# Every fourth expert row of heads 0 to 2: from VectorE to ScalarE and GpSimd

## The chip, the cores and the metric

The kernel runs on one core of a Trainium2 chip. The core has five engines with a queue of instructions each: TensorE (PE in the profile, with its weight loads as PEld), VectorE (DVE), ScalarE (ACT), GpSimd (POOL) and SyncE (SP). They work side by side and meet at semaphores. The metric is the device time of one execution in microseconds (us); lower is better.

## The reference, cut to what matters

The layer is a decoder block: a mixer of attention heads and state-space heads, whose output is added to the residual `h`, and then a PEER channel mixer. For each of 512 tokens and each of 8 heads, PEER picks 16 of 16,384 experts. The picked rows of two tables are then used:

```
u   = expert_down[idx]                       # (tokens, heads, 16, 1024)
pre = einsum('bthkd,btd->bthk', u, xn)
act = gelu(pre) * gates                      # gates: softmax over the 16 picked
out = einsum('bthk,bthkd->btd', act, expert_up[idx])
h   = h + out                                # then a final RMSNorm
```

So each token needs 128 rows of each table, 4 KB each, all in float32. The two tables lie side by side in memory, and one row of the joined table is 8 KB.

## The kernel before, in words

The tokens are worked on in four tiles of 128, one token to a partition. A slot `s` is one picked expert for all 128 tokens of a tile: there are 128 slots to a tile, 16 to a head, 512 in all. GpSimd issues one indirect DMA for each slot (`gather(s)`, L378 to L411), which brings 128 rows of 8 KB, 1.05 MB, into one of ten row buffers (eleven from slot 60 on; `ROW_OF`). A buffer can be filled again when its last user is done with it, and `gather(s)` waits for that.

What happens to a row after it has landed:

- VectorE multiplies its down half by the normed tokens and sums (`dots`, L1049; the instruction is L1053).
- ScalarE takes the gelu of a group of slots (L605), VectorE multiplies by the gates (`gates`, L1058; L1065), and the factors are in `actv`.
- ScalarE makes a diagonal matrix of each factor (L616), and TensorE multiplies it by the up half of the row into the accumulators of the tile (`expert`, L1464; L1477). Its last matmul signals `row_free`.

In the first three heads (`OUT_HEADS` is 3, slots 0 to 47) the slots 3, 7, 11, ... 47 (`SHARE` is 4) take another way: `by_dve(s)` is true, ScalarE and TensorE skip them, and VectorE itself computes `h = row * actv + h` over 128x1024 (`add_row`, L1046). That ends with the signal `row_added`, on which the gather that reuses the buffer waits. It is issued from `dots` of the next group, right behind the first dot product of it. There are 12 such slots. They are in these heads because TensorE has other work there: the output projection of the mixer (`pieces`, L1416), which must end before the gathers of the query weights 5 to 7 begin (L325). The residual with the twelve rows in it is added to the accumulators much later (`add_residual`, L1505).

Head 0's gathers begin at 200 us of the span, while the mixer still runs. From head 3 on (slot 48) GpSimd also makes a diagonal for each slot (`gate_diagonal`, L419), between two gathers.

The order on each engine is written out by hand: what stands behind an instruction that waits, waits too. The names `ring`, `step_ps` and so on belong to the mixer and play no part here. All row buffers, diagonals and small tables are parts of three big tiles, `arena`, `arena2` and `wide`, so that the profile shows most operands under these names.

Of the kernel before, what the change touches and what calls it, by code (L numbers as in the profile page):

```python
# [74 lines left out]

def by_dve(s):

    return s < OUT_HEADS * TOPK and s % SHARE == SHARE - 1

DVE_DONE = list(itertools.accumulate(int(by_dve(s)) for s in range(NS)))
PE_DONE = [s + 1 - DVE_DONE[s] for s in range(NS)]

# [12 lines left out]
def layer(nc, x, x_t, w_in_blocks, w_vd, norm_mix, conv_w, conv_b, dt_bias, a_log, d_skip, ssd_norm_w, sinks, w_out,  # L96
          rel_bias, bucket_line, norm_ffn, w_query, keys1_t, keys2_t, experts_du, norm_cols, out):
    line_dram = nc.dram_tensor("line_scratch", (P, HEADS * LW), F32, kind="Internal").ap()
    with ExitStack() as ctx:
# [239 lines left out]
        def _(gp):  # L339
# [32 lines left out]
            def gate(c):  # L372
# [3 lines left out]
                link(gp, g.tensor_tensor(yb[:, c, :], yb[:, c, :], zs[c], ALU.mult), "gated", n)  # L376

            def gather(s):  # L378
                q, i = divmod(s, TOPK)
# [22 lines left out]
                if s == WIDER:  # L402
                    gp.wait_ge(sem("wo_half"), 2 * NT)
                elif user is not None:
                    if by_dve(user):
                        gp.wait_ge(sem("row_added"), DVE_DONE[user])
                    else:
                        gp.wait_ge(sem("row_free"), PE_DONE[user])
# [37 lines left out]
            gather(11)  # L446
            gather(12)
            gather(13)
            gather(14)
            gather(16)  # L450
            gather(15)
            gather(17)
            gather(18)
            gather(19)
            for s in range(20, NS):
                gather(s)
                if s - 2 >= OUT_HEADS * TOPK:
                    gate_diagonal(s - 2)
# [5 lines left out]
        def _(act):  # L464
# [137 lines left out]
            def group(s0, n_slots):  # L602
                part = slice(s0 % 16, s0 % 16 + n_slots)
                act.wait_ge(sem("dots"), s0 + n_slots)
                nc.scalar.activation(gel[:, part], pre[:, part], ACT.Gelu).then_inc(sem("gelu"), 1)  # L605
                act.wait_ge(sem("act_ready"), N_BEFORE[s0] + 1)
                if s0 == 0:
                    act.wait_ge(sem("off_ps"), NT - 1)
                if s0 == TOPK:
                    act.wait_ge(sem("gated"), 2)  # L610
                for s in range(s0, s0 + n_slots):
                    if by_dve(s):
                        continue
                    if s >= 8:
                        act.wait_ge(sem("row_free"), PE_DONE[s - 8])
                    nc.scalar.activation(diag(s), ident[:], ACT.Copy, scale=actv[:, s % 16:s % 16 + 1]  # L616
                                         ).then_inc(sem("diag"), 1)
# [154 lines left out]
        def _(dve):  # L772
# [266 lines left out]

            def add_row(s):  # L1040

                t = s // SLOTS
                if DVE_DONE[s] > 1:
                    dve.wait_ge(sem("row_added"), DVE_DONE[s] - 1)
                dve.wait_ge(sem("act_ready"), GROUP_OF[s] + 1)
                v.scalar_tensor_tensor(h[:, t, :], rows[ROW_OF[s]][:, D:2 * D], actv[:, s % 16:s % 16 + 1], h[:, t, :],  # L1046
                                       ALU.mult, ALU.add).then_inc(sem("row_added"), 1)

            def dots(s0, n_slots):  # L1049
                for s in range(s0, s0 + n_slots):  # L1050
# [3 lines left out]
                                           pre[:, s % 16:s % 16 + 1]).then_inc(sem("dots"), 1)  # L1054
                    if s == s0 and s and by_dve(s - 1):
                        add_row(s - 1)

# [163 lines left out]
        def _(pe):  # L1221
# [261 lines left out]
            def experts(s0, n_slots):  # L1483
                for s in range(s0, s0 + n_slots):
                    if not by_dve(s):
                        expert(s)
# [18 lines left out]
            def add_residual(t):  # L1505
                pe.wait_ge(sem("h_mixed"), 2 * t + 2)
                if t == 0:
                    pe.wait_ge(sem("row_added"), DVE_DONE[-1])
                for b in range(2):
# [205 lines left out]
```

## Time and profile before

| | |
|---|---|
| median of 3 runs | 1527.85 us (1527.29 to 1528.53) |
| the profiled execution, its own time | 1526.34 us |
| its span, first to last instruction | 1524.5 us |
| PE busy | 1325.1 us, 87% |
| DVE busy | 1053.0 us, 69% |
| ACT busy | 441.6 us, 29% |
| POOL busy | 1108.3 us, 73% |
| mean rate of the DMA engines | 374 GB/s |

The profile is of one execution. Busy shares are means over stages that differ: the mixer fills the first 200 us, and the experts the rest. The profile gives the rate of the DMA engines for 40 equal slices of 38.1 us, and for any stretch that is asked for. Times in the rows are us from the start of the span.

### The profile page before, as it was taken

How to read it: one execution, taken by the hardware profiler on the slowest of the kernel's cores; microseconds unless marked ns; L12 is line 12 of the kernel's file. 1: busy time of each engine (PE TensorE's matmuls, PEld its weight loads, DVE VectorE, ACT ScalarE, POOL GpSimd, SP SyncE). 2: the span in 40 equal slices, each digit the busy share in tenths (PEclk: the TensorE clock that was granted, in tenths of full speed). 3: DMA queues.
4: the chain of work that ended last, by engine and by line, in shares of the span. 5: the costliest groups of instructions: out<-in, count | busy, mean ns of one | idle time of the engine just before them, and what ended most of it. 6: DMA issues, size and time to landing. Idle time of an engine off the chain costs nothing.

```text
span 1524.5 us, 14446 instructions
## 1 busy us (share of the span) xinstructions
PE 1325.1 (87%) x4392; PEld 678.5 (45%) x4392; DVE 1053.0 (69%) x2534; ACT 441.6 (29%) x1216; POOL 1108.3 (73%) x1005
## 2 busy tenths in 40 slices
PE   8999998899888998889889898889888878888886
PEld 5557974444444443444444443434444334434432
DVE  3546598886776777677766676777777676667664
ACT  2123462122323232233223222233233222222222
POOL 0001134548899898888999998888999888888893
PEclk9999999999999999999999999999999999999999
DMA  7640069999999999999999999999999999999995
GB/s 254 172 184 12 1 259 413 412 418 422 421 420 422 421 421 422 421 421 421 421 421 418 421 416 422 422 421 409 408 421 423 420 422 422 421 421 421 416 415 231
DMA packets 85217, 569.80 MB, mean 374 GB/s; under 512 B 10227, under 2 KB 12564, under 8 KB 18708
## 3 DMA queue, kind: packets, MB, share of 16 engines
q0 software_dynamic: 73728, 536.90, 85.1%
q1 hardware_dynamic: 11412, 31.99, 6.2%
q8 instruction: 34, 0.56, 0.1%
q14 instruction: 43, 0.35, 0.1%
HBM read 565.19 MB, written 3.67 MB: 373 GB/s over the span
## 4 chain that ended last, share of the span: by engine, by line
DMA 32%; PE 30%; POOL 21%; DVE 10%; issue 4%; ACT 3%; SPq 0%; DVEq 0%; ACTq 0%; POOLq 0%
DMA arena<-in_experts_du_dram,arena 27%; PE ps L1477 14%; POOL arena L419 11%; POOL arena L409 8%; PE ps L1245 5%; DMA wide<-in_experts_du_dram,arena 5%; PE ps L1416 3%; DVE arena L1053 3%; PE ps L1451 3%; POOL wide L409 2%; ACT arena L647 1%; DVE wide L1053 1%; ACT arena L468 1%; PE ps L1260 1%; PE ps L1232 1%
## 5 line engine op out<-in xcount | busy, mean ns | idle before, releaser
L1477 PE MATMUL ps<-arena 128*128 128x512 f32 x1624 | 774.7, 621 | 141.6 <-ACT arena L647 133.0
L409 POOL DMA_INDIRECT arena<-in_experts_du_dram,arena x418 | 488.0, 1168 | 120.1 <-issue 63.8
L1477 PEld LDWEIGHTS ps<-arena 128*128 128x128 f32 x1624 | 307.3, 196 | 565.7 <-issue 329.9
L419 POOL TENSOR_SCALAR arena<-ident,arena 128x128 f32<-128x128 f32 x464 | 494.8, 1066 | 47.5 <-PE ps L1477 31.9
L1053 DVE CUSTOM_DVE_ANT_0 arena<-arena,wide 128x1024 f32<-128x1024 f32 x210 | 255.3, 1229 | 138.3 <-DMA arena<-in_experts_du_dram,arena 137.5
L1053 DVE CUSTOM_DVE_ANT_0 arena<-arena 128x1024 f32<-128x1024 f32 x208 | 252.6, 1228 | 114.8 <-DMA arena<-in_experts_du_dram,arena 114.1
L643 ACT ACTIVATE arena<-arena 128x2 f32<-128x2 f32 (+1 forms) x234 | 47.5, 203 | 762.0 <-DVE arena L1053 761.7
L1477 PE MATMUL ps<-wide,arena 128*128 128x512 f32 x376 | 183.2, 610 | 29.8 <-ACT arena L647 26.1
L647 ACT ACTIVATE arena<-arena 128x128 f32<-128x128 f32 x464 | 161.1, 394 | 8.1 <-ACT arena L643 0.2
L409 POOL DMA_INDIRECT wide<-in_experts_du_dram,arena x94 | 107.5, 1144 | 60.9 <-DVE arena L1037 24.0
L1477 PEld LDWEIGHTS ps<-wide,arena 128*128 128x128 f32 x376 | 70.0, 194 | 124.8 <-issue 73.6
L357 POOL TENSOR_TENSOR wide<-arena,hrow 128x512 f32<-128x512 f32 x4 | 4.7, 1170 | 116.0 <-ACT arena L468 115.9
L1245 PE MATMUL ps<-arena 128*128 128x512 f32 x192 | 83.4, 593 | 0.0
L1451 PEld LDWEIGHTS ps<-arena,wide 128*128 128x128 f32 x640 | 74.4, 192 | 8.9 <-issue 8.9
L1053 DVE CUSTOM_DVE_ANT_0 wide<-wide 128x1024 f32<-128x1024 f32 x46 | 56.6, 1230 | 30.1 <-DMA wide<-in_experts_du_dram,arena 30.0
L1451 PE MATMUL ps<-arena,wide 128*128 128x128 f32 x640 | 74.8, 275 | 0.0
L1053 DVE CUSTOM_DVE_ANT_0 wide<-wide,arena 128x1024 f32<-128x1024 f32 x48 | 58.8, 1225 | 23.1 <-DMA wide<-in_experts_du_dram,arena 22.9
L468 ACT ACTIVATE arena<-ps 128x256 f32<-128x256 f32 (+1 forms) x109 | 48.6, 446 | 48.0 <-PE ps L1460 14.4
L1416 PE MATMUL ps<-wide,arena 128*128 128x512 f32 x128 | 56.9, 593 | 1.1 <-DVE h L974 1.1
L1245 PEld LDWEIGHTS ps<-arena 128*128 128x128 f32 x192 | 36.1, 190 | 44.3 <-issue 44.2
L1451 PEld LDWEIGHTS ps<-arena 128*128 128x128 f32 x384 | 44.7, 192 | 6.0 <-issue 6.0
L1451 PE MATMUL ps<-arena 128*128 128x128 f32 x384 | 44.9, 275 | 0.6 <-ACT arena L468 0.6
(197 smaller groups left out, 1028.4 us busy)
## 6 DMA issues: line engine op xcount, KB each, us to landing
arena<-in_w_in_blocks_dram SPq DMA_DIRECT2D x16, 512.0 KB, 9.5
arena<-in_experts_du_dram,arena POOLq DMA_INDIRECT x418, 16.4
wide<-in_w_query_dram SPq DMA_DIRECT2D x5, 1024.0 KB, 9.3
wide<-in_w_out_dram SPq DMA_DIRECT2D x1, 4096.0 KB, 17.8
h<-in_x_dram SPq DMA_DIRECT2D x4, 512.0 KB, 9.7
arena<-in_w_query_dram SPq DMA_DIRECT2D x2, 1024.0 KB, 6.4
arena<-in_x_t_dram SPq DMA_DIRECT2D x3, 512.0 KB, 6.5
line_scratch<-arena SPq DMA_DIRECT2D x1, 1536.0 KB
```

The source lines that it names most:

```text
L409: gp.indirect_dma_start(rows[b], None, experts_du, bass.IndirectOffsetOnAxis(ap=idx[:, (q // PH) % 2, q % PH * TOPK + i:q % PH * TOPK + i ...
L419: g.tensor_scalar(diag(s), ident[:], eg[:, q % 2, i:i + 1], None, ALU.mult).then_inc(sem("gate_diag"), 1)
L468: link(act, nc.scalar.activation(o, i, func, **kw), name, n)
L643: nc.scalar.activation(gel[:, part], pre[:, part], ACT.Gelu).then_inc(sem("gelu"), 1)
L647: nc.scalar.activation(diag(s), diag(s), ACT.Copy, scale=gel[:, s % 16:s % 16 + 1]).then_inc(sem("diag"), 1)
L1053: v.tensor_tensor_reduce(down, down, xn2[s // SLOTS % 2], 1.0, 0.0, ALU.mult, ALU.add, pre[:, s % 16:s % 16 + 1]).then_inc(sem("dots"), 1)
L1232: last = mm(ps[0][:, t * P:(t + 1) * P], ring[:, 0, k, :], xnT[:, t, k, :], start=(k == 0), stop=(k == KT - 1))
L1245: last = mm(bank[:].rearrange("p (t c) -> p t c", t=NT), ring[:, ring_slot(b), k, :], xnT[:, :, k, :], start=(k == 0), stop=(k == KT - 1))
L1260: last = mm(ps[z_bank(t)][:, i * P:(i + 1) * P], xnT[:, t, k, :], ring[:, ring_slot(NXB + 5 + i), k, :], start=(k == 0), stop=(k == KT - 1))
L1416: ins = mm(ps[out_bank(c, b)][:], mixT[c][:, k, :], wo[:, k, b * 512:(b + 1) * 512], start=(k == 0), stop=(k == KT - 1), skip_group_check= ...
L1451: last = mm(ps[query_bank(q)][:, j * P:(j + 1) * P], w[:, k, j, :], xn2T[:, k, :], start=(k == 0), stop=(k == KT - 1))
L1477: last = mm(acc(t, b)[:], diag(s), up[:, b * 512:(b + 1) * 512], start=(s % SLOTS == 0), stop=False, skip_group_check=True)
```

## The change

The twelve rows are scaled by ScalarE in their buffer (a Copy with a scale, 128x1024), which signals `up_scaled`; GpSimd then adds the scaled row to `h` (a tensor_tensor, 128x1024) and signals `row_added`. VectorE's `add_row` is gone. `by_dve` and `DVE_DONE` are renamed.

```diff
-def by_dve(s):
+def by_pool(s):
     return s < OUT_HEADS * TOPK and s % SHARE == SHARE - 1
...
+            def add_row(s):                       # on GpSimd
+
+                t = s // SLOTS
+                gp.wait_ge(sem("up_scaled"), POOL_DONE[s])
+                gp.wait_ge(sem("h_mixed"), 2)
+                link(gp, g.tensor_tensor(h[:, t, :], h[:, t, :], rows[ROW_OF[s]][:, D:2 * D], ALU.add), "row_added", n)
...
             gather(12)
+            add_row(3)
             gather(13)
...
             gather(15)
+            add_row(7)
             gather(17)
...
             for s in range(20, NS):
                 gather(s)
+                if by_pool(s + 1 - RING_E):
+                    add_row(s + 1 - RING_E)
                 if s - 2 >= OUT_HEADS * TOPK:
                     gate_diagonal(s - 2)
...
                 for s in range(s0, s0 + n_slots):  # group(), on ScalarE
-                    if by_dve(s):
+                    if by_pool(s):
+                        up = rows[ROW_OF[s]][:, D:2 * D]
+                        nc.scalar.activation(up, up, ACT.Copy, scale=actv[:, s % 16:s % 16 + 1]
+                                             ).then_inc(sem("up_scaled"), 1)
                         continue
...
-            def add_row(s):                       # on VectorE
-                t = s // SLOTS
-                if DVE_DONE[s] > 1:
-                    dve.wait_ge(sem("row_added"), DVE_DONE[s] - 1)
-                dve.wait_ge(sem("act_ready"), GROUP_OF[s] + 1)
-                v.scalar_tensor_tensor(h[:, t, :], rows[ROW_OF[s]][:, D:2 * D], actv[:, s % 16:s % 16 + 1], h[:, t, :],
-                                       ALU.mult, ALU.add).then_inc(sem("row_added"), 1)
...
                     v.tensor_tensor_reduce(down, down, xn2[s // SLOTS % 2], 1.0, 0.0, ALU.mult, ALU.add,
                                            pre[:, s % 16:s % 16 + 1]).then_inc(sem("dots"), 1)
-                    if s == s0 and s and by_dve(s - 1):
-                        add_row(s - 1)
```

GpSimd's queue before, from the gather of slot 15 to that of slot 21 (in these rows `row_free` is TensorE's signal for a buffer, `row_added` that of the twelve rows):

```order
L409 DMA arena2<-in_experts_du_dram,arena 128x2048 [waits row_free]
L409 DMA arena<-in_experts_du_dram,arena 128x2048 [waits row_added]
L409 DMA arena<-in_experts_du_dram,arena 128x2048 [waits row_free] x2
L409 DMA wide<-in_experts_du_dram,arena 128x2048 [waits row_free]
L409 DMA arena<-in_experts_du_dram,arena 128x2048 [waits row_added]
```

The same piece of the queue now; L416 is the gather, L383 the addition of a row:

```order
L416 DMA arena2<-in_experts_du_dram,arena 128x2048 [waits row_free]
L383 TENSOR_TENSOR h<-h,arena 128x1024 [waits h_mixed,up_scaled]
L416 DMA arena<-in_experts_du_dram,arena 128x2048 [waits row_added]
L416 DMA arena<-in_experts_du_dram,arena 128x2048 [waits row_free] x2
L416 DMA wide<-in_experts_du_dram,arena 128x2048 [waits row_free]
L383 TENSOR_TENSOR h<-h,arena 128x1024 [waits h_mixed,up_scaled]
L416 DMA arena<-in_experts_du_dram,arena 128x2048 [waits row_added]
```

The rows of slots 7 and 11 are now added on GpSimd itself, each right ahead of the gather that reuses its buffer (slots 17 and 21), and the other gathers stand behind them.

Farther on, GpSimd's queue before, from the gather of slot 48 (it waits `routed`, the indices of the next head) to the diagonal of slot 49; L419 is a diagonal:

```order
L409 DMA arena<-in_experts_du_dram,arena 128x2048 [waits row_free,routed]
L409 DMA arena<-in_experts_du_dram,arena 128x2048 [waits row_added]
L409 DMA wide<-in_experts_du_dram,arena 128x2048 [waits row_free]
L419 TENSOR_SCALAR arena<-ident,arena 128x128 [waits row_free,gates_ready]
L409 DMA arena<-in_experts_du_dram,arena 128x2048 [waits row_free]
L419 TENSOR_SCALAR arena<-ident,arena 128x128 [waits row_free]
```

And the same piece now, up to the gather of slot 53; L426 is a diagonal:

```order
L416 DMA arena<-in_experts_du_dram,arena 128x2048 [waits row_free,routed]
L383 TENSOR_TENSOR h<-h,arena 128x1024 [waits h_mixed,up_scaled]
L416 DMA arena<-in_experts_du_dram,arena 128x2048 [waits row_added]
L416 DMA wide<-in_experts_du_dram,arena 128x2048 [waits row_free]
L426 TENSOR_SCALAR arena<-ident,arena 128x128 [waits row_free,gates_ready]
L416 DMA arena<-in_experts_du_dram,arena 128x2048 [waits row_free]
L426 TENSOR_SCALAR arena<-ident,arena 128x128 [waits row_free]
L416 DMA arena<-in_experts_du_dram,arena 128x2048 [waits row_free]
L383 TENSOR_TENSOR h<-h,arena 128x1024 [waits h_mixed,up_scaled]
L426 TENSOR_SCALAR arena<-ident,arena 128x128 [waits row_free,row_added]
L416 DMA arena<-in_experts_du_dram,arena 128x2048 [waits row_added]
```

The rows of slots 39 and 43 are added here, behind the gathers of slots 48 and 52; a third addition (slot 47) stands behind the gather of slot 56.

On ScalarE the scaling (L625) stands behind the three diagonals (L630) of its group, and ahead of the next gelu (L616):

```order
L616 ACTIVATE arena<-arena 128x4
L630 ACTIVATE arena<-ident,arena 128x128 x3
L625 ACTIVATE arena<-arena 128x1024
L610 ACT_TABLE_LOAD
L610 ACTIVATE arena<-arena 128x16
L616 ACT_TABLE_LOAD
```

## Rows read from the trace of the kernel before

**Rows 1.** The page: rate of the DMA engines in 40 slices; the gathers' queue.
```profile
GB/s 254 172 184 12 1 259 413 412 418 422 421 420 422 421 421 422 421 421 421 421 421 418 421 416 422 422 421 409 408 421 423 420 422 422 421 421 421 416 415 231
...
q0 software_dynamic: 73728, 536.90, 85.1%
```
**Rows 2.** The page, DMA issues: count, median us from issue to landing.
```profile
arena<-in_experts_du_dram,arena POOLq DMA_INDIRECT x418, 16.4
```
**Rows 3.** Stretches of 2 us: PE, PEld, DVE, ACT, POOL busy, PEclk, DMA share, GB/s.
```profile
264.00:266.00 2.00, 2.00 (x6) 0.83 (x5) 1.73 (x5) 0.90 (x4) 1.27 (x2) 1.00 0.95 299
266.00:268.00 2.00, 2.00 (x6) 0.88 (x5) 2.00 (x4) 0.29 (x1) 1.22 (x2) 1.00 0.93 385
268.00:270.00 2.00, 2.00 (x6) 0.95 (x5) 1.10 (x3) 0.00 (x0) 1.39 (x3) 1.00 0.91 307
270.00:272.00 2.00, 1.67 (x4) 0.38 (x2) 0.88 (x2) 0.00 (x0) 1.70 (x2) 1.00 1.01 348
...
328.00:330.00 2.00, 2.00 (x6) 0.95 (x5) 1.90 (x4) 0.49 (x2) 0.93 (x1) 1.00 1.02 365
```
**Rows 4.** Long stretches, L409 alone: gathers' time (count), PEclk, DMA share, GB/s.
```profile
195.00:263.25 68.25, 24.67 (x22) 0.97 0.89 357
...
195.00:334.49 139.49, 55.30 (x50) 0.98 0.95 384
195.00:341.20 146.20, 59.18 (x53) 0.98 0.95 386
```
**Rows 5.** Timeline of SyncE's DMA queue: query weights.
```profile
193.56 0.80 SPq L319 DMA_DIRECT2D arena<-in_w_query_dram  x2
288.75 0.86 SPq L323 DMA_DIRECT2D arena<-in_w_query_dram  x2
```
**Rows 6.** The chain that ended last: start, us, what.
```profile
245.20 9.56 DMA arena<-in_experts_du_dram,arena
254.79 1.24 DVE arena L1053 x2
...
259.40 5.41 PE ps L1477 x8
...
305.87 1.25 DVE arena L1053 x2
...
308.78 0.23 DVE arena L1065
...
309.49 7.11 PE ps L1477 x12
```
**Rows 7.** GpSimd's timeline: start, us, line, [idle before it, until what].
```profile
253.41 0.94 POOL L409 DMA_INDIRECT arena<-in_experts_du_dram,arena  x1 [0.30 <-issue]
263.25 1.10 POOL L409 DMA_INDIRECT arena<-in_experts_du_dram,arena  x1 [8.90 <-PE ps L1477]
...
330.74 0.94 POOL L409 DMA_INDIRECT arena<-in_experts_du_dram,arena  x1 [1.72 <-DVE arena L1037]
```
**Rows 8.** Line L1046, the removed addition: ns min/median/max, first and last start.
```profile
L1046 DVE SCALAR_TENSOR_TENSOR h<-arena,h x12: 1273/1280/1382, 230.8 to 343.1; 128x1024 f32<-128x1024 f32 x12
```
**Rows 9.** Tile h: ScalarE over 128x1024, same columns.
```profile
L468 ACT ACTIVATE wide<-h x2: 1040/1040/1041, 406.1 to 1052.1; 128x1024 f32<-128x1024 f32 x2
```
**Rows 10.** Groups on GpSimd: busy us, mean ns | idle before and releasers.
```profile
L376 POOL TENSOR_TENSOR wide<-wide,arena 128x512 f32<-128x512 f32 x4 | 5.1, 1271 | 40.9 <-DVE arena L819 34.5 <-DVE wide L928 6.4
L357 POOL TENSOR_TENSOR wide<-arena,hrow 128x512 f32<-128x512 f32 x4 | 4.7, 1170 | 116.0 <-ACT arena L468 115.9
```
**Rows 11.** GpSimd's timeline at 98 us.
```profile
97.91 1.04 POOL L357 TENSOR_TENSOR wide<-arena,hrow 128x512 f32<-128x512 f32 x1 [94.70 <-ACT arena L468]
```
**Rows 12.** VectorE's timeline over the same time.
```profile
98.03 1.47 DVE L884 TENSOR_TENSOR arena<-arena,dtv 128x512 f32<-128x512 f32 x1
99.53 0.69 DVE L888 TENSOR_TENSOR arena<-arena,dec 128x512 f32<-128x512 f32 x1
```
**Rows 13.** Line L419, GpSimd's diagonals: ns min/median/max.
```profile
L419 POOL TENSOR_SCALAR arena<-ident,arena x464: 593/793/2524, 336.4 to 1501.9; 128x128 f32<-128x128 f32 x155
```

More of the change, by code:

```diff
@@ L73 @@
 LOADS_IN_RING = [1 + sum(ring_slot(i) == ring_slot(n) for i in range(n)) for n in range(NBLK)]
-def by_dve(s):
+def by_pool(s):
     return s < OUT_HEADS * TOPK and s % SHARE == SHARE - 1
-DVE_DONE = list(itertools.accumulate(int(by_dve(s)) for s in range(NS)))
-PE_DONE = [s + 1 - DVE_DONE[s] for s in range(NS)]
+POOL_DONE = list(itertools.accumulate(int(by_pool(s)) for s in range(NS)))
+PE_DONE = [s + 1 - POOL_DONE[s] for s in range(NS)]
 ROW_OF = [s % RING_E if s < WIDER else (s - WIDER - 1) % (RING_E + 1) for s in range(NS)]
@@ L404, in gather @@
                 elif user is not None:
-                    if by_dve(user):
-                        gp.wait_ge(sem("row_added"), DVE_DONE[user])
+                    if by_pool(user):
+                        gp.wait_ge(sem("row_added"), POOL_DONE[user])
                     else:
@@ L1484, in experts @@
                 for s in range(s0, s0 + n_slots):
-                    if not by_dve(s):
+                    if not by_pool(s):
                         expert(s)
@@ L1507, in add_residual @@
                 if t == 0:
-                    pe.wait_ge(sem("row_added"), DVE_DONE[-1])
+                    pe.wait_ge(sem("row_added"), POOL_DONE[-1])
                 for b in range(2):
```

## The prediction, made before the run

> **What bounds the kernel now.** I read the DMA rate over the whole span first. From the seventh slice (229 us) to the last but one it stands at 408 to 423 GB/s [rows 1], and no engine is as full as that. Of the 569.8 MB of the page 536.9 MB are the gathers' 512 rows of 1.05 MB [rows 1], 2.49 us each at 422 GB/s. The kernel is a stream of DMA with compute beside it: a microsecond costs time when the DMA engines have nothing asked of them, and a delay elsewhere costs nothing as long as requests are queued. In the long middle a gather lands 16.4 us after it is issued (median) [rows 2], so six or seven rows are queued, and four or five microseconds of delay on GpSimd would pass unseen.
>
> The change acts only in slots 0 to 47, from 230 to about 355 us. There I looked for the stretches in which the rate falls. In steps of 2 us there are two: 264 to 272 us with 299, 385, 307 and 348 GB/s instead of 422, and 328 to 330 us with 365 [rows 3]. The first is (123 + 37 + 115 + 74) x 2 / 422 = 1.7 us lost, the second 0.3 us. All that a better feeding of the queue could win here is 2.0 us.
>
> Why the first is there, the chain of waits says [rows 6]: a row issued at 245.2 lands at 254.8, its dot product ends at 256, a search follows, TensorE starts the experts of slots 12 to 14 at 259.4, and only then is the buffer for slot 22 free. GpSimd issues slot 21 at 253.4, waits 8.9 us for TensorE and issues slot 22 at 263.25 [rows 7]. How full the queue was follows from two counts: by 263.25 us 68.25 us x 357 GB/s = 24.4 MB had moved [rows 4], and asked were 22 gathers (23.1 MB) and two blocks of query weights (2.1 MB) [rows 4, 5]. 0.8 MB, 1.9 us, was left. The same count gives 2.0 MB at 334.5 us (50 gathers and three blocks against 139.5 us x 384 GB/s) and 2.3 MB at 341.2 us [rows 4, 5], 4.8 and 5.4 us of work: nowhere near the 16 us of later.
>
> **What goes.** VectorE loses 12 additions of 1.28 us, 15.4 us [rows 8]. Does an end hang on them? The rows of the chain wait in turn for a row's landing (254.8 us) and for TensorE (309.5 us and on, which works through pieces and experts without a pause). The additions stand ahead of those waits, so VectorE would be early and wait longer. I count 0, and 2.0 us gained as the end of the range, if earlier gates keep the queue full at both dips.
>
> **What is added on ScalarE.** 12 scalings of 128x1024, 1.04 us each by the nearest row [rows 9], 12.5 us. They stand behind the diagonals that TensorE needs and ahead of a gelu that waits for VectorE's next dot products; ScalarE is 29% busy. I count 0; were one to stand in front of a gelu it would be 1.0 us at that place.
>
> **What is added on GpSimd.** 12 tensor_tensors of 128x1024 with both inputs in SBUF. The trace has none of that size. 128x512 took 1.27 us with two full inputs and 1.04 at best with a broadcast one [rows 10, 11]; twice that is 2.1 to 2.54 us, and I take 2.4. The Trainium skill's GPSIMD Engine Reference (section "Performance versus the Vector engine") has 4497 ns for 2048 elements, which would be an estimated 2.25 us for half of them; places 1, 2 and 4 would be some 0.15 us cheaper for each addition, half a microsecond in all.
>
> That is the bare price. The dearer part is that such an addition and VectorE hold each other up. At 97.91 us GpSimd starts a tensor_tensor of 1.04 us, and VectorE's two-input instruction of 98.03 us takes 1.47 us, where the next one of the same shape takes 0.69 [rows 11, 12]: 0.78 us longer, and it ends 0.55 us behind GpSimd's. The other way round, GpSimd's diagonals take 0.59 us at best, 0.79 in the median and up to 2.52 [rows 13], so one can wait nearly 1.9 us. The dot products (down half and tokens) and the gates have two SBUF inputs as well. So an addition can last 2.4 to 4.3 us in its queue, and stop VectorE for up to 2.4 us where it begins first. The Trainium skill's page SBUF — State Buffer, section "Who interferes with whom", states it as a lock: a VectorE instruction with two SBUF inputs and a GpSimd instruction that reads SBUF exclude each other, and the second blocks until the first ends; the trace agrees at 98 us, with its 0.78 us.
>
> Against the 1.28 us saved on VectorE thus stand up to 2.4 us of blocked VectorE for each row, and 2.4 to 4.3 us of GpSimd's queue, in which the gathers stand. By place:
>
> 1. The addition of slot 11, behind the gather of slot 20. It stands where slot 21 was issued before, at 253.41 [rows 7]; slot 7's addition ahead of it, less what GpSimd's waits for TensorE take up of it, shifts it by my estimate to 254 to 255.5 us. The dot product that the chain needs starts at 254.79 [rows 6]. If the addition is first, the dot product, the gates and slot 22 come about 1.9 us later, with an empty queue: 1.9 us. If the dot product is first, nothing, since a search of one-input instructions follows. I take 1.0.
> 2. The addition of slot 15, between the gathers of slots 24 and 25, in the stretch from 268 us. Slot 25 and the ones behind it come 2.4 us later, in the stretch that is already starved (307 and 348 GB/s). 0 to 2.4 us; since slots 22 to 24 are queued by then, 0.7.
> 3. The addition of slot 31, behind the gather of slot 40, by my estimate near 307 us. The gates that start TensorE's long run stand at 308.78, the dot product before them ends at 307.1 [rows 6]. An addition that begins there ends at 309.4: 0.6 us late; up to 1.7. TensorE then runs without a pause until slot 48, and slot 46, whose issue comes just before the second dip, goes with it. I take 0.6.
> 4. The additions of slots 39, 43 and 47, behind the gathers of slots 48, 52 and 56 (the first at 330.74 us [rows 7], the last by 354). GpSimd is now full: three additions of 2.4 to 3.2 us in front of diagonals and gathers, 7 to 10 us, against 4.8 and 5.4 us queued. Slot 49 would be issued at 334.4 to 336.3 us (330.74 + 0.94 + 0.3 + 2.4 to 4.3) instead of 332. From the 2.0 MB the 3 us take 1.3, and the next additions the rest; when the projection's pieces end, three query weights of 1 MB fill the queue again. 0 to 3 us; I take 1.3.
>
> The earlier additions (slots 3 and 7) delay slots that wait for TensorE anyway or have two rows queued before them: 0, up to 0.5 each. The others (slots 19, 23, 27, 35) fall where three to five rows are queued: 0.
>
> Sum: 1.0 + 0.7 + 0.6 + 1.3 = 3.6 us. Ends: -2.0, and 1.9 + 2.4 + 1.7 + 3.0 + 1.0 = 10 us if all go wrong. A loss here is not won back, because from 355 us on the DMA rate is at its top. Against the profiled execution's own 1526.34 us (span 1524.5 and 1.8 around it) this is 1529.9; the median of the runs is 1.5 us above that execution, so 1527.85 + 3.6 = 1531.5 us.
>
> **Rivals.** (a) The additions are absorbed. For it: only about 2 MB short of full anywhere, and the dips of before cost 1.7 and 0.3 us although the queue was nearly dry, so small gaps are cheap. Against it: place 4 asks more of GpSimd than it has. Time: 0 to 2.5 us more, about 1528.8. (b) VectorE's relief reaches the dip at 264 us: with three additions fewer before 256 us the gates of slots 12 to 15 come up to 1.28 us earlier, slot 22 too, and the queue does not run dry. It decides if the dot product at 254.79 was late for VectorE's sake; the row says it waited for a landing, which speaks against it. Price: -1.3 us, with the second dip -2.0, so 1525.9 to 1526.6. Only with an unforeseen gain of the same kind would it be seen as faster. (c) The blocking is stronger than I took: each of 12 additions waits the full 1.9 us and blocks VectorE for 2.4, places 1 to 4 all at their upper end: 1536 to 1538. (d) That the twelve rows still go through VectorE is excluded by the order.
>
> **How the numbers follow.** Forecast 3 to 7 us slower: 0.45. Rival (a): 0.38. Rival (b): 0.10. Rival (c): 0.07. A measurement of this kernel can tell 0.2%, 3.1 us, from no change. Slower by more than that: nearly all of the forecast's case and (c), 0.50. Faster by more: half of (b), 0.06. Within: 0.44. The range for 8 in 10 goes from 1526.5, in (b), to 1536.5, the edge of (c); the forecast's own is 1530.5 to 1534.5.
>
> **What would show it.** The additions on GpSimd at 2.2 to 2.6 us where VectorE is idle and above 3 where it is not; dot products of 2 to 3.5 us beside them, against 1.23; slot 22 issued at 263.3 or, if place 1 holds, near 265; a rate under 400 GB/s at 336 to 354 us, where the slices have 418 and 422 [rows 1]; GpSimd without idle time from 331 to 358 us; and from 360 us on the same course as before, shifted by the loss. The forecast is wrong if the rate at 336 to 354 us stays at 420 (place 4), or if the first dip shrinks (then rival b).

## The result, and the profile after

The changed kernel took 1534.97 us in the median (1534.48 to 1540.67, six runs), the kernel before 1527.16 (1525.0 to 1528.53, six runs beside them). The ratio is 1.0064, with a 95% interval of [1.0051, 1.0076]: 7.8 us slower by the medians, where 3.65 were forecast (the ratio by itself would be 9.8 us). A second series of the same kernel, made with the experiments, gave 1535.51 us (1531.34 to 1537.58) and 1.0049 [1.0036, 1.0063]. The profiled execution of the first series took 1540.67 us (span 1538.9, mean granted clock 0.968), 14.3 us more than the one of before, and is thus the longest of the runs; the profile of the second took 1535.67 us. What is read from one of them alone says so. Losses in us are from here on differences of medians against the kernel before in the same series; two runs, of 1559.9 us (last three additions) and 2019.6 us (the same, only writing), had a granted clock of 0.85 and 0.62 and are left out of the ratios, not of the medians, which they move by 0.3 us.

The page of the changed kernel, the share and the rate of the DMA engines in 40 slices (38.5 us each), to be laid beside [rows 1]:

```profile
DMA  7640079999999999999999999999999999999995
GB/s 251 173 186 6 1 275 380 371 370 382 421 421 422 421 421 421 422 421 421 421 422 422 421 421 422 421 421 422 421 411 421 421 420 422 421 421 408 413 414 241
```

Slices 7 to 10 (from 231 to 385 us) had 413, 412, 418 and 422 GB/s and have 380, 371, 370 and 382. Together that is 162 GB/s less for 38.3 us (the mean slice of the two), 14.7 us at 422 GB/s: the whole of this execution's 14.3. All four slices are low, not only the one of place 4. From 385 us on the course is the old one.

The same in the stretches in which the groups of additions stand, of the changed kernel (columns as [rows 3]):

```profile
229.00:267.00 38.00, 28.16 (x89) 14.19 (x88) 30.38 (x59) 11.76 (x24) 20.73 (x16) 0.91 0.97 385
267.00:305.00 38.00, 33.27 (x70) 14.05 (x70) 31.18 (x62) 9.50 (x22) 21.59 (x16) 0.87 0.95 377
305.00:336.00 31.00, 26.39 (x84) 13.76 (x83) 25.14 (x45) 9.84 (x21) 20.61 (x15) 0.89 0.97 372
336.00:360.00 24.00, 24.00 (x57) 10.64 (x56) 19.80 (x47) 6.46 (x14) 18.89 (x14) 1.00 0.95 357
```

and of before:

```profile
229.00:267.00 38.00, 33.09 (x99) 16.37 (x98) 31.75 (x71) 8.73 (x23) 16.09 (x15) 0.96 1.00 413
267.00:305.00 38.00, 33.48 (x96) 15.85 (x95) 31.77 (x72) 5.81 (x17) 19.39 (x18) 1.00 1.01 412
305.00:336.00 31.00, 27.97 (x75) 13.25 (x74) 24.77 (x51) 8.38 (x19) 10.50 (x10) 0.94 1.01 416
336.00:360.00 24.00, 23.97 (x56) 10.26 (x54) 17.66 (x47) 7.14 (x19) 20.36 (x21) 1.00 1.01 424
```

In order these are 2.5, 3.2, 3.2 and 3.8 us of transfers missing. VectorE's busy time in them is 106.5 us against 106.0, although 15.4 us of additions are gone and this execution is by then behind with the rest of its work: something fills the time they left.

What fills it, two timelines of the changed kernel show, GpSimd's first (start, us, instruction; in brackets the idle time before it and what ended it):

```profile
234.68 2.36 POOL L383 TENSOR_TENSOR h<-h,arena 128x1024 f32<-128x1024 f32 x1
237.81 1.15 POOL L416 DMA_INDIRECT arena<-in_experts_du_dram,arena  x1 [0.77 <-POOL h L383]
...
249.78 2.51 POOL L383 TENSOR_TENSOR h<-h,arena 128x1024 f32<-128x1024 f32 x1
253.06 1.14 POOL L416 DMA_INDIRECT arena<-in_experts_du_dram,arena  x1 [0.77 <-POOL h L383]
...
257.98 2.35 POOL L383 TENSOR_TENSOR h<-h,arena 128x1024 f32<-128x1024 f32 x1
...
282.17 2.35 POOL L383 TENSOR_TENSOR h<-h,arena 128x1024 f32<-128x1024 f32 x1
...
317.72 2.34 POOL L383 TENSOR_TENSOR h<-h,arena 128x1024 f32<-128x1024 f32 x1
```

And VectorE's beside those five additions:

```profile
234.81 3.33 DVE L1058 CUSTOM_DVE_ANT_0 arena<-arena 128x1024 f32<-128x1024 f32 x1 [2.30 <-DMA arena<-in_experts_du_dram,arena]
...
248.86 1.22 DVE L1058 CUSTOM_DVE_ANT_0 arena<-arena 128x1024 f32<-128x1024 f32 x1
...
250.19 3.18 DVE L1058 CUSTOM_DVE_ANT_0 wide<-wide,arena 128x1024 f32<-128x1024 f32 x1
...
257.32 4.10 DVE L1058 CUSTOM_DVE_ANT_0 arena<-arena 128x1024 f32<-128x1024 f32 x1 [3.94 <-DMA arena<-in_experts_du_dram,arena]
...
282.09 2.47 DVE L1040 TENSOR_SCALAR arena<-arena 128x16 f32<-128x16 f32 x1
...
318.01 2.08 DVE L1068 SCALAR_TENSOR_TENSOR arena<-arena 128x4 f32<-128x4 f32 x1 [3.55 <-ACT arena L616]
```

A dot product takes 1.22 us when alone. Beside an addition it takes 3 to 4, and ends 1.10, 1.08 and 1.09 us after the addition's own end (234.81 + 3.33 = 238.14 against 237.04, and so on): it stands still nearly to the end of the addition and then does its work. Gates and a `tensor_scalar` of a search, 0.2 us each, end 0.03 to 0.05 us after it. The additions themselves last 2.34 to 2.51 us. In this execution an instruction of VectorE is held beside each of the twelve, 0.4 to 2.9 us each. The first eleven sum to 22 us, against the 15.4 us that VectorE was relieved of.

The chain that ended last, in the changed kernel (start, us, what; before it is [rows 6]):

```profile
234.81 4.49 DVE arena L1058 x4
...
248.42 8.87 DMA arena<-in_experts_du_dram,arena
257.32 4.11 DVE arena L1058 x2
...
264.81 3.79 PE ps L1480 x4
...
274.53 4.20 DVE arena L1058 x4
...
282.09 2.47 DVE arena L1040
...
288.18 13.47 PE ps L1419 x24
...
318.01 2.09 DVE arena L1068
...
320.58 7.50 PE ps L1480 x12
```

Five held instructions of VectorE stand in it: the dot products at 234.81, at 257.32 (slot 15's) and at 274.53, the `tensor_scalar` at 282 us and the gates at 318. TensorE's long run begins at 320.58 instead of 309.49.

### The profile page after: what moved, and what is told of

The parts are those of the page before. It is cut to its first block, busy times and chain, and to the rows that moved or that the text cites. A ratio compares the mean times of both kernels' runs of the same rounds, so it can differ in the third digit from the quotient of the medians.

```text
span 1538.9 us, 14471 instructions
## 1 busy us (share of the span) xinstructions
PE 1332.8 (87%) x4392; PEld 681.0 (44%) x4392; DVE 1061.6 (69%) x2522; ACT 454.1 (30%) x1228; POOL 1128.7 (73%) x1017
## 4 chain that ended last, share of the span: by engine, by line
DMA 34%; PE 31%; POOL 19%; DVE 9%; issue 4%; ACT 3%; SPq 0%; DVEq 0%; POOLq 0%; ACTq 0%
DMA arena<-in_experts_du_dram,arena 27%; PE ps L1480 15%; POOL arena L426 9%; POOL arena L416 7%; DMA wide<-in_experts_du_dram,arena 7%; PE ps L1248 5%; DVE arena L1058 4%; PE ps L1454 4%; PE ps L1419 2%; POOL wide L416 2%; ACT arena L479 1%; ACT arena L661 1%; PE ps L1235 1%; PE ps L1263 0%; PE ps L1271 0%
## 5 line engine op out<-in xcount | busy, mean ns | idle before, releaser
L416 POOL DMA_INDIRECT arena<-in_experts_du_dram,arena x418 | 485.1, 1161 | 108.2 <-issue 61.6
L426 POOL TENSOR_SCALAR arena<-ident,arena 128x128 f32<-128x128 f32 x464 | 487.7, 1051 | 56.2 <-PE ps L1480 40.7
L1058 DVE CUSTOM_DVE_ANT_0 arena<-arena 128x1024 f32<-128x1024 f32 x208 | 262.9, 1280 | 120.4 <-DMA arena<-in_experts_du_dram,arena 119.9
L1480 PE MATMUL ps<-wide,arena 128*128 128x512 f32 x376 | 185.1, 616 | 33.8 <-ACT arena L661 29.5
L416 POOL DMA_INDIRECT wide<-in_experts_du_dram,arena x94 | 109.1, 1161 | 57.8 <-DVE arena L1051 24.8
L1058 DVE CUSTOM_DVE_ANT_0 wide<-wide,arena 128x1024 f32<-128x1024 f32 x48 | 62.8, 1308 | 21.2 <-DMA wide<-in_experts_du_dram,arena 21.0
L1419 PE MATMUL ps<-wide,arena 128*128 128x512 f32 x128 | 59.8, 618 | 3.1 <-DVE h L988 3.1
## 6 DMA issues: line engine op xcount, KB each, us to landing
wide<-in_w_out_dram SPq DMA_DIRECT2D x1, 4096.0 KB, 17.8
```

Source lines behind the costliest of these rows:

```text
L416: gp.indirect_dma_start(rows[b], None, experts_du, bass.IndirectOffsetOnAxis(ap=idx[:, (q // PH) % 2, q % PH * TOPK + i:q % PH * TOPK + i ...
L426: g.tensor_scalar(diag(s), ident[:], eg[:, q % 2, i:i + 1], None, ALU.mult).then_inc(sem("gate_diag"), 1)
L1058: v.tensor_tensor_reduce(down, down, xn2[s // SLOTS % 2], 1.0, 0.0, ALU.mult, ALU.add, pre[:, s % 16:s % 16 + 1]).then_inc(sem("dots"), 1)
L1419: ins = mm(ps[out_bank(c, b)][:], mixT[c][:, k, :], wo[:, k, b * 512:(b + 1) * 512], start=(k == 0), stop=(k == KT - 1), skip_group_check= ...
L1480: last = mm(acc(t, b)[:], diag(s), up[:, b * 512:(b + 1) * 512], start=(s % SLOTS == 0), stop=False, skip_group_check=True)
```

## The experiments

All were timed in five rounds beside the kernel before. In the edits `ON_DVE` is the list of the slots, out of the twelve, that VectorE scales and adds as before; the others are scaled by ScalarE and added by GpSimd as in the change. These edits also keep the additions to `h` in order: one on either engine waits for the ones before it on the other. In two kernels this stops VectorE for some time, which is told there.

**The additions left out.** Everything of the change stays but the sum: GpSimd writes one column of the row and signals, so the twelve rows are missing from `h`.

```diff
-link(gp, g.tensor_tensor(h[:, t, :], h[:, t, :], rows[ROW_OF[s]][:, D:2 * D], ALU.add), "row_added", n)
+link(gp, gp.memset(rows[ROW_OF[s]][:, D:D + 1], 0.0), "row_added", n)
```

> From the changed kernel; the twelve rows are scaled by ScalarE, but GpSimd only writes one column of the row and signals, so the twelve additions are left out. VectorE has no addition either. Theory S (GpSimd's addition stops VectorE while it runs): all of the 7.8 us goes, 1527 us. Theory Q (the additions' 2.36 us and the 0.77 us behind each stand in the gathers' queue): also 1527 us. If VectorE's relief of 12 x 1.28 us is worth something, it is seen here alone: 1525 to 1526 us; if it is worth nothing, 1527.

Measured 1526.06 us, ratio 0.9991 [0.9982, 1.0000]. VectorE's relief and ScalarE's scalings together are worth a gain of 1.5 us by the medians, 0 to 2.7 by the interval. All of the loss comes with GpSimd's additions.

**GpSimd as long busy, but only writing.** Three memsets of 128x1024 in place of each addition (0.96 us each, 2.99 for the three; the twelve rows are left out of `h`, and the up half is overwritten).

```diff
-link(gp, g.tensor_tensor(h[:, t, :], h[:, t, :], rows[ROW_OF[s]][:, D:2 * D], ALU.add), "row_added", n)
+up = rows[ROW_OF[s]][:, D:2 * D]
+for _ in range(NFILL - 1):                    # NFILL = 3
+    link(gp, gp.memset(up, 0.0), "filled", n)
+link(gp, gp.memset(up, 0.0), "row_added", n)
```

> From the changed kernel; in place of each addition GpSimd fills the up half of the row three times in succession (write only, no SBUF input), about 3 us of its queue by 205 ns for 128x128, and the twelve additions are left out. Theory S: writes do not stop VectorE's dot products, which stay at 1.22 us: 1527 to 1529 us. Theory Q: the gathers stand behind the same time as before: 1533 to 1536 us.

Measured 1531.41 us, 1.0023 [1.0014, 1.0032]: 3.8 us, between what the two theories had. With the 0.77 us in which a gather right behind waits for the last one's signal, three memsets keep the queue for 3.76 us, longer than the addition's 3.13 (2.36 and the same 0.77), and cost half of the additions' 7.8. At least some half of the loss is thus not GpSimd's time.

**ScalarE scales, VectorE adds.** The scaling stays on ScalarE, the addition goes back to VectorE at its old place.

```diff
-link(gp, g.tensor_tensor(h[:, t, :], h[:, t, :], rows[ROW_OF[s]][:, D:2 * D], ALU.add), "row_added", n)
+v.tensor_tensor(h[:, t, :], rows[ROW_OF[s]][:, D:2 * D], h[:, t, :], ALU.add).then_inc(sem("row_added"), 1)
```

> ScalarE scales the twelve rows as in the changed kernel, and VectorE adds them (tensor_tensor, at the place of the addition of the kernel before). Both theories: ScalarE's 12 x 1.13 us are hidden, 1527 us (+0 to 1). A third one, that the scaling delays gelus or diagonals: 1529 us or more.

Measured 1527.87 us, 1.0001 [0.9992, 1.0011]. The 12 scalings (1.13 us each) cost nothing that can be measured.

**Which additions cost it.** First two that were to settle the early places: all but slot 3 on GpSimd, and only slot 11.

```diff
+ON_DVE = (3,)
...
+ON_DVE = (3, 7, 15, 19, 23, 27, 31, 35, 39, 43, 47)
```

> The row of slot 3 goes through VectorE as in the kernel before, the other eleven through ScalarE and GpSimd. Theory S with the first place dear (the addition at 234.7 us holds a dot product for 3.3 us, the gates of slots 4 to 7 come 3.3 us later and the queue runs dry at 248 us): 2 to 3.5 us of the 7.8 come back, 1531.5 to 1533 us. Theory Q: one twelfth comes back, 0.6 us, 1534.3 us.

Measured 1536.42 us, 1.0054 [1.0041, 1.0068]: nothing came back.

> The kernel before, with the row of slot 11 alone scaled by ScalarE and added by GpSimd; the other eleven stay on VectorE. Theory S (VectorE stopped): the addition falls on the dot product of slot 15, which takes over 3 us, the gates of slots 12 to 15 and the gather of slot 22 come up to 2.9 us later into a queue that is nearly dry: 2 to 3 us slower, 1529.5 to 1530.5 us. Theory Q (queue time): one addition is a twelfth of 3.8 us: 0.3 us. A third, that the dot product of slot 15 starts first and so keeps its 1.23 us: no change.

Measured 1527.58 us, 0.9999 [0.9990, 1.0008]: nothing was lost. The dot product of slot 15 came late enough to be held for half a microsecond only; VectorE's and GpSimd's timelines of this kernel:

```profile
255.84 1.76 DVE L1087 CUSTOM_DVE_ANT_0 arena<-arena 128x1024 f32<-128x1024 f32 x1 [3.75 <-DMA arena<-in_experts_du_dram,arena]
```

```profile
254.16 2.34 POOL L397 TENSOR_TENSOR h<-h,arena 128x1024 f32<-128x1024 f32 x1
```

What both runs were expected to show if stops of VectorE were dear failed; no change had also been named for the second, but for a dot product that starts first, and this one did not. Place 1, as the prediction priced it, is not there when slot 11's addition is alone.

**The three groups, each alone.** Slots 3, 7 and 11; slots 15 to 35; slots 39, 43 and 47.

```diff
+ON_DVE = (15, 19, 23, 27, 31, 35, 39, 43, 47)
...
+ON_DVE = (3, 7, 11, 39, 43, 47)
...
+ON_DVE = (3, 7, 11, 15, 19, 23, 27, 31, 35)
```

> The kernel before, with the rows of slots 3, 7 and 11 alone on ScalarE and GpSimd. The difference between the changed kernel (+7.8) and the one with these three on VectorE (+5.0 us) says 2.8 us: 1530.5 us, if the places add up. Slot 11 alone cost nothing; by theory S that is because slots 3 and 7 bring its addition ahead of a dot product or make the queue dry at 248 to 256 us: then 2 to 4 us. If the three cost nothing here, 1527.7 us, they only cost together with the later ones.

Measured 1532.24 us (1528.52 to 1534.32), 1.0037 [1.0023, 1.0051]: 5.1 us, more than either branch of the expectation. The profiled execution took 1528.52 us, the shortest of the six; in it slot 15's dot product is not held, so what the longer ones met is not seen.

> The kernel before, with the rows of slots 15, 19, 23, 27, 31 and 35 on ScalarE and GpSimd. What is left of the 7.8 us after 2.8 for slots 3 to 11 and 3.5 for slots 39 to 47 is 1.5 us: 1529 us. My prediction had 0.7 for slot 15 and 0.6 for slot 31: 1.3 us, the same. If the places do not add up: 1527.7 or over 1531 us.

Measured 1531.23 us, 1.0029 [1.0018, 1.0041]: more than was expected.

> The kernel before, with the rows of slots 39, 43 and 47 alone on ScalarE and GpSimd. The prediction's place 4 had 1.3 us for them (0 to 3): 1528.5 to 1529.5 us, with a DMA rate that falls under 400 GB/s between 336 and 354 us. If the loss in this place needs the delays of the places before it, no change: 1527.5 us.

Measured 1531.19 us, 1.0023 [1.0014, 1.0032], more than was expected. GpSimd's timeline at the second of its additions:

```profile
343.00 1.00 POOL L432 DMA_INDIRECT arena<-in_experts_du_dram,arena  x1 [0.17 <-issue]
344.02 2.36 POOL L397 TENSOR_TENSOR h<-h,arena 128x1024 f32<-128x1024 f32 x1
346.48 2.53 POOL L442 TENSOR_SCALAR arena<-ident,arena 128x128 f32<-128x128 f32 x1
349.18 1.55 POOL L432 DMA_INDIRECT arena<-in_experts_du_dram,arena  x1 [0.17 <-issue]
```

VectorE beside it:

```profile
343.78 3.70 DVE L1087 CUSTOM_DVE_ANT_0 arena<-arena 128x1024 f32<-128x1024 f32 x1
```

And the stretch as a whole:

```profile
336.00:360.00 24.00, 22.37 (x53) 9.76 (x52) 19.46 (x39) 5.32 (x12) 21.29 (x19) 1.00 0.89 335
```

The addition holds the dot product, and then the diagonal behind the addition takes 2.53 us instead of 0.79 [rows 13]: two gathers are 6.2 us apart. That GpSimd was now full, as the prediction said, shows here: 21.29 of these 24 us busy. The three groups alone lose 5.1, 4.1 and 3.5 us, 12.7 together, where all twelve lose 7.8.

Slots 3, 7 and 11 back on VectorE, with nine on GpSimd, was run against the same question:

```diff
+ON_DVE = (3, 7, 11)
```

> The changed kernel, with the rows of slots 3, 7 and 11 on VectorE as before and the other nine on GpSimd. If the dot products held up at slots 6, 14 and 15 are what is dear: 3 to 5 us of the 7.8 come back, 1530 to 1532 us. If slots 15 to 47 are: at most 1 us comes back, 1534 to 1535 us.

Measured 1532.31 us, 1.0035 [1.0023, 1.0047]: 4.6 us. The changed kernel had 1535.51 in the same series, so the first three add 3.2 us when they come on top, and cost 5.1 when they are alone. The losses of groups do not add.

**The same groups, only writing.** The edit of three memsets, in the groups (the rows of the group are left out of `h`).

> As the kernel with slots 3, 7 and 11 alone on GpSimd (5.1 us slower), but with three fills of the up half (write only, 3.76 us of the queue) in place of each addition; these three additions are left out. Theory S: VectorE's dot products stay at 1.2 us and at most 1 us is left, 1527 to 1528.5 us. Theory Q: 4 to 5 us slower, 1531.5 us.

Measured 1527.81 us, 1.0003 [0.9994, 1.0011].

> As the kernel with slots 15 to 35 on GpSimd (4.1 us slower), but with three fills in place of each addition; these six additions are left out. Theory S: at most 1.5 us is left, 1528.5 us. Theory Q: 4 us slower, 1531 us.

Measured 1527.55 us, 1.0006 [0.9997, 1.0014].

> As the kernel with slots 39, 43 and 47 alone on GpSimd (3.5 us slower than before), but in place of each addition GpSimd fills the up half three times (3 x 0.96 us, write only; these three additions are left out). Theory Q at this place (queue time): the same 3 to 4 us slower, 1531 us, since the fills are 0.6 us longer than an addition. Theory S: VectorE's dot product of slot 48, which took 3.70 us beside an addition, is at 1.22 us and most of the loss goes: 1528 us.

Measured 1529.39 us, 1.0015 [1.0005, 1.0025]. For the first two groups the loss goes when GpSimd only writes. Their dot products are no longer held, as the line's shortest, median and longest show; first slots 15 to 35 by additions, then by memsets:

```profile
L1087 DVE CUSTOM_DVE_ANT_0 arena<-arena x208: 1209/1224/3358, 225.7 to 1197.1; 128x1024 f32<-128x1024 f32 x104
```

```profile
L1090 DVE CUSTOM_DVE_ANT_0 arena<-arena x208: 1210/1225/1476, 222.4 to 1190.7; 128x1024 f32<-128x1024 f32 x104
```

For the last group 2.3 us of 3.5 remain (the two intervals overlap), and the rate of its stretch says the same, 374 GB/s with memsets (335 with additions, 424 before):

```profile
336.00:360.00 24.00, 23.93 (x56) 10.26 (x54) 15.98 (x46) 8.21 (x20) 21.88 (x23) 1.00 0.98 374
```

**How many additions it takes at the start.** Slot 3 alone, slot 7 alone, slots 3 and 7:

```diff
+ON_DVE = (7, 11, 15, 19, 23, 27, 31, 35, 39, 43, 47)
...
+ON_DVE = (3, 11, 15, 19, 23, 27, 31, 35, 39, 43, 47)
...
+ON_DVE = (11, 15, 19, 23, 27, 31, 35, 39, 43, 47)
```

> The kernel before, with the row of slot 3 alone on ScalarE and GpSimd. My prediction counted it at 0, up to 0.5 us: 1527.5 us. The profile of the changed kernel shows the addition beside the dot product of slot 6, which takes 3.33 us, and the gates of slots 4 to 7 3.3 us later: by theory S the queue then runs dry near 246 us and it costs 1.5 to 3 us: 1529 to 1530 us.

Measured 1527.67 us, 1.0005 [0.9996, 1.0014]; a miss.

> The kernel before, with the row of slot 7 alone on ScalarE and GpSimd. Slots 3 and 11 alone cost nothing, the three together 5.1 us. If slot 7 is the dear one by itself: 2 to 5 us slower. By the theory that a single stop of VectorE is swallowed by the requests queued, and only stops that follow on each other reach the DMA engines: within 1 us of before, 1527.5 to 1528.5 us.

Measured 1528.09 us, 1.0005 [0.9996, 1.0014].

> The kernel before, with the rows of slots 3 and 7 on ScalarE and GpSimd. By the theory that stops add up once the first has used up what was queued: 2 to 4 us slower, 1529.5 to 1531.5 us, with a DMA rate under 400 GB/s between 229 and 267 us. If slot 11 is what the three need: no change.

Measured 1528.81 us, 1.0014 [1.0005, 1.0023]: 1.9 us, under the expected range. One addition costs nothing that can be measured (slot 11 alone neither), two cost 1.9 us and three 5.1. This is not a clean series. In the last two kernels no instruction of VectorE stands beside slot 7's addition. VectorE waits instead, by the order that the edit keeps, before it may add slot 11's row: 3.26 us with slot 7 alone, and here

```profile
252.46 1.28 DVE L1080 SCALAR_TENSOR_TENSOR h<-arena,h 128x1024 f32<-128x1024 f32 x1 [4.45 <-POOL h L397]
```

The changed kernel has no such wait. And the profile of slot 3 alone already has the rate of the changed kernel (385 GB/s) in the first stretch, though its median is only 0.2 us above before:

```profile
229.00:267.00 38.00, 31.28 (x86) 15.30 (x87) 28.93 (x61) 8.07 (x19) 16.51 (x14) 0.87 0.97 385
```

**The changed kernel once more.** No edit.

> The changed kernel once more. Its times so far lie in two groups (1534.5 to 1535.1 and 1539.2 to 1540.7 us), and the profile is of the upper one. If the profile falls in the lower group, it shows which of the places differs: by theory S the time that TensorE's pieces take from 288 us (13.5 us in the upper group's profile against 10.5 before, at a lower granted clock) is 3 us shorter, or one dot product is not held up. Median 1535 to 1536 us.

Measured as told above. In this profile (GpSimd's timeline, then VectorE's) the addition of slot 11 again begins near 257.7 us, but slot 15's row has landed 1.7 us earlier and its dot product is done:

```profile
257.68 2.35 POOL L383 TENSOR_TENSOR h<-h,arena 128x1024 f32<-128x1024 f32 x1
260.81 1.50 POOL L416 DMA_INDIRECT arena<-in_experts_du_dram,arena  x1 [0.77 <-POOL h L383]
264.88 1.02 POOL L416 DMA_INDIRECT arena<-in_experts_du_dram,arena  x1 [2.57 <-PE ps L1480]
```

```profile
255.62 1.22 DVE L1058 CUSTOM_DVE_ANT_0 arena<-arena 128x1024 f32<-128x1024 f32 x1 [3.13 <-DMA arena<-in_experts_du_dram,arena]
```

Slot 22 is issued at 264.88, against 268.86 in the longer execution and 263.25 before. Which instructions are held differs between the two executions; that goes with a spread of 9 us over the twelve runs of the changed kernel (1531.3 to 1540.7), where the kernel before has 3.5 to 5.8 in a series.

**Three rows given to TensorE instead.** An attempt at a better kernel: before, with slots 15, 19 and 23 on the ordinary way.

```diff
-    return s < OUT_HEADS * TOPK and s % SHARE == SHARE - 1
+    return s < OUT_HEADS * TOPK and s % SHARE == SHARE - 1 and s not in (15, 19, 23)
```

> A version that may beat both: the kernel before, with the rows of slots 15, 19 and 23 taken by TensorE like their neighbours and not by VectorE (nine on VectorE). TensorE stands idle before and after these groups, each costs it 1.7 us, and VectorE is relieved of 3 x 1.28 us. The kernel that left all additions out was 1.5 us faster than the one before; 0 to 1 us of that is to be had here: 1526.5 to 1527.5 us. If TensorE's 5.1 us delay the release of buffers at 264 us, slower: 1529 us.

Measured 1526.65 us, 0.9995 [0.9986, 1.0004]: no gain that can be measured. No run with the whole computation beat the kernel before.

## Why the prediction was half right

The frame held. The time is lost where the DMA engines have nothing asked of them, and the four slices account for it. The relief of VectorE, set at 0, is worth 1.5 us by the medians (0 to 2.7); the scalings on ScalarE, set at 0, cost nothing that can be measured, at 1.134 us instead of the 1.04 of [rows 9]. An addition is 2.36 us, 2.4 predicted. Direction and mechanism (additions that hold VectorE, and, with the last three alone, a GpSimd that is full in place 4) are shown. The size was off by a factor of two, in these steps:

1. "The earlier additions (slots 3 and 7) delay slots that wait for TensorE anyway or have two rows queued before them: 0, up to 0.5 each." This is the step that failed most. With place 1 the prediction had 1.0 us for slots 3, 7 and 11, and as a group they cost 5.1. Priced one by one the 0 is right within the noise (the intervals of the three single runs end at 1.2 to 2.1 us). But in the changed kernel each held VectorE for 2 us and GpSimd for 3 while little was queued, and the first stop may spend what the second was to live on. This reading is not shown: with slot 3 back on VectorE nothing came back (1536.42 us), and the run with two additions has a wait of its own. Shown are the 5.1 us of the three together, and that they go when GpSimd only writes. How little was queued, the count shows with which the prediction began, here at the gather of slot 16 (columns as [rows 4]), in the changed kernel:

```profile
195.00:246.50 51.50, 15.97 (x15) 1.00 0.86 333
```

and before:

```profile
195.00:243.20 48.20, 15.95 (x15) 1.00 0.84 330
```

Asked in both are 15 gathers and two blocks of query weights, 17.8 MB. Before, 15.9 MB (48.20 us x 330 GB/s) had moved by 243.2 us, and 1.9 MB were queued when slot 16 was issued at 243.30. Now 17.15 MB had moved by 246.50, and 0.7 MB (1.6 us) were left when it was issued at 246.53. What follows is a dip where before had 422 to 426 GB/s, ahead of the one of place 1 (steps of 2 us, changed kernel):

```profile
246.00:248.00 2.00, 2.00 (x20) 2.00 (x20) 1.73 (x6) 0.37 (x2) 1.48 (x1) 1.00 0.97 406
248.00:250.00 2.00, 2.00 (x14) 1.54 (x14) 2.00 (x3) 1.98 (x5) 1.68 (x3) 1.00 0.67 188
250.00:252.00 2.00, 2.00 (x6) 0.95 (x5) 1.90 (x3) 1.97 (x4) 2.00 (x1) 1.00 0.90 356
252.00:254.00 2.00, 2.00 (x6) 0.88 (x5) 1.38 (x2) 0.79 (x1) 1.23 (x2) 1.00 0.96 279
```

2. Place 1, "I take 1.0". The order of the two instructions does vary, as the prediction said, but not with the consequence it gave. It counted the case "dot product first" as free. In the longer execution the dot product's record began at 257.32, 0.66 us ahead of the addition's, and took 4.10 us; the gates behind it came at 264.09 (258.69 before) and slot 22 at 268.86. As the only addition it cost nothing, and with slots 3 and 7 ahead of it 3.4 us (1532.24 against 1528.81). In other profiles too, dot products that had begun up to 0.47 us ahead were held.

3. "Nothing, since a search of one-input instructions follows." The searches are not free of it.
4. "The others (slots 19, 23, 27, 35) fall where three to five rows are queued: 0", with 0.7 for slot 15 and 0.6 for slot 31. Slots 15 to 35 cost 4.1 us as a group and nothing when GpSimd only writes for as long. Depth of the queue shields from a late gather; it does not shield a TensorE that waits for gates, whose buffers then come free late. That this is the path is read from the chain: the dot product at 274.53 and the `tensor_scalar` at 282.09 are held by the additions of slots 15 and 19 and stand ahead of TensorE's pieces at 288.18, the gates at 318.01 by that of slot 31. I had followed it at slot 31 alone.

5. Place 4, "I take 1.3", ends 0 and 3.0: it is 3.5 alone, at or above the upper end (2.1 to 4.9 by the interval). Two items were missing from GpSimd's time: 0.77 us behind the first of the three additions until its own signal lets the next gather go (behind the other two stands a diagonal, after 0.1 us), and a 2.53 us diagonal, beside VectorE's delayed dot products. By the medians two thirds remain with memsets, so here GpSimd's time is likely the greater part.

6. "An addition can last 2.4 to 4.3 us in its queue" fell. None was over 2.71 us in any profile; nearly all the waiting is VectorE's. That error made the forecast dearer in GpSimd's time and cheaper in VectorE's.

7. "A loss here is not won back" holds as far as can be told. In the second profile the rates from 229 to 400 us miss 11.8 us, and that execution is 9.3 longer; 2.3 of the difference are two slices of before with 409 and 408 GB/s [rows 1] that this execution did not have. The sum is rough: by 229 us this execution had moved 1.6 us more (150 GB/s against 147).

Rival (c) had about the right size (1536 to 1538), but each of its two halves was wrong by itself: the additions do not wait, and the places are more than four. The prediction has no term for TensorE's clock, and both profiles of the changed kernel show that it falls more often (mean granted clock 0.91, 0.87 and 0.89 in the first three stretches above, before 0.96, 1.00 and 0.94). In the longer execution TensorE, after 3.06 us without work, is granted 0.50 of full speed (the 1.2 GHz level) from 288 to 294 us, and 24 matmuls of the projection take 13.47 us, against 10.54 before.

```profile
288.00:294.00 6.00, 5.82 (x7) 2.50 (x8) 5.97 (x8) 0.00 (x0) 5.42 (x3) 0.50 1.00 422
```

In the second profile these 24 take 10.30 us, but the 12 expert matmuls ahead of them, after 3.42 us without work, 8.40 (mean clock 0.64), where before had 5.42 at full clock after 3.45; first the second profile, then before:

```profile
277.69:286.09 8.40, 8.39 (x13) 3.63 (x14) 7.99 (x20) 1.84 (x4) 6.38 (x5) 0.64 0.99 399
```

```profile
275.12:280.54 5.42, 5.41 (x12) 2.19 (x12) 5.10 (x15) 0.80 (x3) 2.80 (x3) 1.00 1.02 431
```

Four groups of TensorE in the chain of the second profile stand behind such a wait (2.49 to 4.83 us) and take 7.13, 6.59, 8.39 and 8.25 us, where as many matmuls at full clock take 5.15 (12) and 3.45 (8). By my estimate that is 11.5 us over; before has two such groups (5.41 and 7.11 us), 3.9 over. The difference, 7.5 us, stands in a chain of an execution that is 9.3 us longer, so the clock may carry much of what a held VectorE starts. No run here separates it from the rest.

Open remain the split of place 4 between the held dot products and the held diagonals, and how much of the missing sum (12.7 against 7.8) each pair of groups shares. A half-width addition on GpSimd, which could have said whether the loss goes with the length of a hold, was not tried.

## What to carry to other kernels

Work moved to GpSimd beside a busy VectorE is to be priced by what it holds up: count every VectorE instruction with two SBUF inputs, and every one-input `tensor_scalar` or cast, that can fall in its 2.4 us, and take up to its whole length as lost on VectorE there (0.4 to 2.9 us here). Where a queue of transfers covers delays, do not price the stops one by one and add: the additions of slots 3 and 11 alone cost nothing that could be measured, three together cost 5.1 us, and three groups that cost 12.7 us one by one cost 7.8 together. A write-only filler at least as long as the moved operation tells time in the queue from contention. Where an experiment splits a sum over two engines, look for the waits that keep their order: they are a stop that the kernel in question does not have.

## What was not expected of the hardware

- The one that begins first does not always go on. In the pairs of dot product and addition over ten profiles the dot product was held whenever it began at most 0.66 us before the addition's record or after it, and ended 1.08 to 1.10 us behind the addition. Where it had begun 0.71 to 0.98 us before, it took its 1.22 us, and the addition 2.49 to 2.71 instead of 2.35. The Trainium skill's page SBUF — State Buffer, section "SBUF: two separate sides", has it that whichever starts first gets the ports; by the records' starts the slot 15 pair disagrees. Why is open.
- A gather right behind an addition starts 0.77 us after it ends, since it waits for the addition's signal (ten of the twelve in the changed kernel). The same holds behind a memset. This is not in the busy time of either.
- Memsets of 128x1024 on GpSimd (0.96 us) left the dot products beside them at no more than 1.48 us.
